# Adding the experts' rows to x by accumulating DMAs, and one more expert by one-hot products

## The chip, the cores and the metric

The kernel runs on one core of a Trainium2 chip. The core has a matrix engine (TensorE, PE in the profile), a vector engine (VectorE, DVE), an activation engine (ScalarE, ACT), a general engine (GpSimd, POOL) and an engine that issues transfers (SyncE, SP). Each engine runs its own queue of instructions; semaphores order them among each other. Transfers run on 16 DMA engines, whichever engine issued them. The metric is the device time of one execution in microseconds, the median of several runs.

## The reference

One decoder layer in float32 over 512 tokens of width 1024: a front part (attention and a recurrent mixer), an output projection, then a mixture of experts and a last norm. Only the last part matters here:

```python
logits = (xf @ router_w + router_b)          # 512 tokens, 32 experts
top_val, top_idx = lax.top_k(logits, 4)      # each token goes to 4 experts
gates = softmax(top_val)
# for each expert e, over the tokens that chose it:
gu = xb @ mlp1_w[e] + mlp1_b[e]              # 1024 -> 2048
act = (up + 1.0) * gate * sigmoid(1.702 * gate)
y = act @ mlp2_w[e] + mlp2_b[e]              # 1024 -> 1024
# the output:
x = x + sum over the token's 4 experts of gate * y
return rmsnorm(x, final_norm_w)
```

## The kernel before, in words

The kernel has three blocks: `front`, `output_and_route`, and `experts`. The change is in the third, but for one line.

**Rounds.** `experts` handles up to 128 rows of each expert in one round, and there can be four rounds, for the case that an expert was chosen by more than 128 tokens. Every engine has a `run(r)` with its whole work of a round. The helper `rounds` (L1382 to 1386) loops over four rounds; in each it loads a flag from the tile `flags` into a register (L1384) and branches over the body if the flag is not set (L1385). With these inputs one round is run and three are skipped. SP alone runs its first round (`rest(0)`, L1423) outside that loop.

**An expert's pieces.** The weights come in as pieces of 1 MB: eight pieces for the product up, four (`DOWN`) for the product down. SP loads them into six slots of `raw` (L1395), each as soon as VectorE has finished with the piece six before. ScalarE rounds each piece to float32r (`split`, L1491, into `w_pieces_hi`), VectorE takes the rest (`split`, L1597, into `w_pieces_lo`), and TensorE makes three products of parts for each piece (L1775, L1778 for up, L1796, L1801 for down). The turn `b` of the steady loop does the product down of expert b-2 and the product up of expert b. After the loop the product down of expert 30 (turn 32, into banks 4 and 5) and of expert 31 (turn 33, into banks 0 and 1) are left.

**Rows in and out.** GpSimd gathers an expert's rows of the normed x (`gather`, L1445), and scatters the gated results `ys` (written by ScalarE, L1511) into rows of `y_dram`, called expert_rows in the profile (`scatter`, L1457), at row 4 * token + (which of the token's four choices). After each scatter it waits for the landing (L1459). `y_dram` was filled with zeros in `front` (L344). `SCATTERED` is 31: experts 0 to 30 are scattered. Expert 31 isn't: its 128 rows are brought to their tokens on TensorE. The one-hot matrix of its tokens (`sel`, made by VectorE with an is_equal, L1603) is turned (L1852), copied to `sel_t` (L1568), and multiplied with the high and low part of the gated result (`y_hi` by ScalarE L1577, `y_lo` by VectorE L1701, products in `choose`, L1875), on top of the bias of the product down (`down_bias`, L1870).

**The end.** When the last scatter has landed, SP (which waits at L1410) loads 16 tiles of 512 KB from `y_dram`, four for each of the four tiles of 128 tokens (L1416), into `raw` and `o_t`. For each tile of tokens, in the order `LAST_ROWS` = 0, 3, 1, 2, VectorE adds in five instructions the four loads, x, and the sum in PSUM (L1717, L1720, L1723, L1726, L1728); ScalarE squares and sums the row (L1581) and takes the root (L1583); VectorE inverts it (L1707) and scales by it and by the weight (`finish`, L1711); SP stores the tile (L1419). `finish(n-1)` stands behind the five additions of tile n. After that SP (L1420) and VectorE (L1732) wait for the stores and GpSimd (L1477) for the last scaling, and only then do they skip the three other rounds. The block ends with a DRAIN on each engine and a barrier (L171).

Of the kernel before, what the change touches and what calls it, by code (L numbers as in the profile page):

```python
# [19 lines left out]
F32 = mybir.dt.float32  # L20
# [3 lines left out]
ALU = mybir.AluOpType  # L24
# [3 lines left out]
P = 128  # L28
# [16 lines left out]
SCATTERED = EXPERTS - 1  # L45
# [990 lines left out]
def output_and_route(nc, d, sb, sem, st, g, con, ident, psum, bank):  # L1036
# [124 lines left out]
    def _(dve):  # L1161
# [81 lines left out]
        nc.vector.tensor_tensor(rank[:, :, INDEXED - 1:INDEXED], which[:, :, EXPERTS - 1:EXPERTS], ranks[:, :, EXPERTS - 1:EXPERTS], ALU.add)  # L1243
# [89 lines left out]
def experts(nc, d, sb, sem, st, g, con, ident, psum, bank, out):  # L1333
# [31 lines left out]
    s_row = [[sem(f"row_loaded{t}_{k}") for k in range(4)] for t in range(NT)]  # L1365
    s_fw, s_add, s_sum, s_ss, s_sd, s_rs, s_o, s_out = (sem(n) for n in ("final_w_loaded", "rows_added", "rows_summed", "x3_squared",
                                                                         "x3_deviation", "x3_rstd", "out_ready", "out_stored"))
    sel_t = xh[:, 0:NT, :].rearrange("p a b -> p (a b)")
    y_hi, y_lo = (a[:].rearrange("p a b -> p (a b)") for a in (ah, al))
    fw, final = xg, (uu, sg, av, ys)  # L1370
    gate_last = tab[:, EXPERTS - 1, 2:3]
    rows_v = y_dram.rearrange("(t p k) n -> t p k n", p=P, k=4)
    last_banks = {0: 2, 3: 6, 1: 4, 2: 0}

    def row(t, k):

        return raw[:, 2 * t + k // 2, k % 2, :] if t < 3 else o_t[:, 2 * k:2 * k + 2, :].rearrange("p a s -> p (a s)")
# [4 lines left out]
    def rounds(eng, run):  # L1382
        with eng.Fori(0, ROUNDS) as r:
            flag = eng.value_load(flags[0:1, bass.ds(r, 1)])  # L1384
            with eng.If(flag == 1):  # L1385
                run(r)

    @block.sync
    def _(sp):
# [7 lines left out]
        def rest(r):  # L1397
# [22 lines left out]
            sp.wait_ge(s_out, (r * NT + NT) * 16)  # L1420
            sp.sem_inc(s_part, 1)

        rest(0)  # L1423
        with sp.Fori(1, ROUNDS) as r:
            flag = sp.value_load(flags[0:1, bass.ds(r, 1)])
            with sp.If(flag == 1):
                for p in range(DOWN, DOWN + RAW):
                    load(r, 0, p)
                rest(r)

    @block.gpsimd
    def _(pool):
# [29 lines left out]
        def run(r):  # L1462
# [14 lines left out]
            pool.wait_ge(s_o, r * NT + NT)  # L1477
            pool.sem_inc(s_part, 1)

        rounds(pool, run)  # L1480

    @block.scalar
    def _(act):
# [50 lines left out]
        def run(r):  # L1534
# [32 lines left out]
            act.wait_ge(s_st, r + 1)  # L1567
            nc.scalar.activation(sel_t, bank(7), ACT.Copy).then_inc(s_selt, 1)  # L1568
# [6 lines left out]
            y_out(r, b - 2, b)  # L1575
            act.wait_ge(s_used, r * STREAM + (STREAM + RING))
            nc.scalar.activation(y_hi, psum[:, 0:2, :].rearrange("p b n -> p (b n)"), ACT.Copy, scale=gate_last).then_inc(s_y, 1)  # L1577
            nc.scalar.activation(stat[:, 52:53], con("eps"), ACT.Sqrt)
            for n, t in enumerate(LAST_ROWS):
                act.wait_ge(s_sum, r * NT + (n + 1))  # L1580
                nc.scalar.activation(row(t, 0), final[t][:], ACT.Square, accum_out=stat[:, 40 + t:41 + t]).then_inc(s_ss, 1)  # L1581
# [3 lines left out]
        rounds(act, run)  # L1585

    @block.vector
    def _(dve):
# [66 lines left out]
        def run(r):  # L1655
# [39 lines left out]
            for p in range(DOWN - 1):  # L1695
                split(r, b + 1, p)
            a_lo(r, b - 1, 1, 7)
            split(r, b + 1, DOWN - 1)
            nc.vector.tensor_scalar(rank[:], rank[:], float(-P), None, ALU.add).then_inc(s_round, 1)
            dve.wait_ge(s_y, r * EXPERTS + (EXPERTS + 1))  # L1700
            nc.vector.scalar_tensor_tensor(y_lo, psum[:, 0:2, :].rearrange("p b n -> p (b n)"), gate_last, y_hi.bitcast(F32),  # L1701
                                           ALU.mult, ALU.subtract).then_inc(s_yl, 1)

            def finish(n):
# [6 lines left out]
                nc.vector.scalar_tensor_tensor(final[t][:], final[t][:], stat[:, 48 + t:49 + t], fw[:], ALU.mult, ALU.mult).then_inc(s_o, 1)  # L1711

            for n, t in enumerate(LAST_ROWS):
                f = final[t][:]
                for k in range(2):
                    dve.wait_ge(s_row[t][k], r * 16 + 16)
                nc.vector.tensor_tensor(f, row(t, 0), row(t, 1), ALU.add).then_inc(s_add, 1)  # L1717
                dve.wait_ge(s_row[t][2], r * 16 + 16)
                dve.wait_ge(s_add, r * 4 * NT + (4 * n + 1))
                nc.vector.tensor_tensor(f, f, row(t, 2), ALU.add).then_inc(s_add, 1)  # L1720
                dve.wait_ge(s_hot, r * NT + (n + 1))
                summed = psum[:, last_banks[t]:last_banks[t] + 2, :].rearrange("p b n -> p (b n)")
                nc.vector.tensor_tensor(x[:, t, :], summed, x[:, t, :], ALU.add).then_inc(s_add, 1)  # L1723
                dve.wait_ge(s_row[t][3], r * 16 + 16)
                dve.wait_ge(s_add, r * 4 * NT + (4 * n + 2))
                nc.vector.tensor_tensor(f, f, row(t, 3), ALU.add).then_inc(s_add, 1)  # L1726
# [11 lines left out]
    def _(pe):  # L1738
# [89 lines left out]
        def run(r):  # L1828
# [52 lines left out]
            for t in LAST_ROWS[:3]:  # L1881
                down_bias(t)
# [47 lines left out]
```

## Time and profile before

| what | value |
|---|---|
| median of 3 runs | 1749.18 us (1747.82 to 1750.51) |
| the profiled execution | 1748.68 us |
| its span, first to last instruction | 1746.8 us |
| TensorE busy | 1589.4 us, 91% of the span |
| VectorE busy | 1423.9 us, 82% |
| ScalarE busy | 1052.6 us, 60% |
| first instruction of `experts` / last of VectorE | 519.2 us / 1737.8 us |

The span is what the profile shows of one execution; the time of that execution has 1.9 us more around it. Where a stretch is full on TensorE, a delay of TensorE is a delay of everything behind it; in the last 45 us the queue that sets the end changes several times, so that stretch has to be read instruction by instruction.

### The profile page before, as it was taken

Reading aid. Unit: us, or ns where it says so; the run is one execution under the profiler, and the core shown is the slowest. Engines: PE = TensorE matmul, PEld = TensorE weight load, DVE = VectorE, ACT = ScalarE, POOL = GpSimd, SP = SyncE. Lnnn points to the kernel's source line nnn. Section 1 sums busy time; section 2 is a strip of 40 time slices with the busy share of each in tenths; the row PEclk is TensorE's granted clock in tenths of the full one; section 3 lists DMA queues with packets and bytes.
Section 4 is the critical chain, followed back from the end, with each engine's and each line's share of the span. In section 5 each row is a group of like instructions: output and inputs, shape, how many; then the busy total and the mean of one; then the engine's idle time right before and its main releaser. Section 6 shows DMA issues by size and latency. Waiting matters only on the chain.

```text
span 1746.8 us, 28600 instructions
## 1 busy us (share of the span) xinstructions
PE 1589.4 (91%) x10300; PEld 1279.4 (73%) x10301; DVE 1423.9 (82%) x1296; ACT 1052.6 (60%) x968; POOL 309.6 (18%) x208
## 2 busy tenths in 40 slices
PE   5888889886877999999999999999999999999991
PEld 5666657665665788888888888888888888888880
DVE  4757667475637799999999999999999999999976
ACT  5434242322335677777777777777777777777761
POOL 6200000000001031122211222122321213222210
PEclk9999899998878999999999999999999999999995
DMA  5610011000547699999999999999999999999956
GB/s 185 242 38 25 26 37 38 26 1 2 208 169 287 241 363 370 361 357 367 358 381 372 349 375 369 371 368 347 368 363 368 352 359 368 364 359 361 358 207 248
DMA packets 100824, 467.62 MB, mean 268 GB/s; under 512 B 12734, under 2 KB 39374, under 8 KB 51488
## 3 DMA queue, kind: packets, MB, share of 16 engines
q1 hardware_dynamic: 88336, 438.11, 66.3%
q0 software_dynamic: 12432, 28.70, 4.4%
q8 instruction: 43, 0.70, 0.2%
q14 instruction: 13, 0.11, 0.0%
HBM read 454.88 MB, written 28.84 MB: 277 GB/s over the span
## 4 chain that ended last, share of the span: by engine, by line
PE 65%; DVE 1%; issue 1%; DMA 1%; ACT 1%; SPq 0%; DVEq 0%; POOL 0%; POOLq 0%; ACTq 0%
PE psum L1775 27%; PE psum L1778 13%; PE psum L1796 13%; PE psum L1801 6%; PE psum L1767 2%; PE psum L1757 2%; PE psum L1787 1%; PE psum L1748 1%; DMA o_t<-expert_rows 1%; ACT w_pieces_hi L1491 0%; DMA expert_rows<-ys,this_i 0%; DMA xg<-h_rows,gath_i 0%; DVE xl L1614 0%; DVE w_pieces_lo L1597 0%; SPq L1416 0%
## 5 line engine op out<-in xcount | busy, mean ns | idle before, releaser
L1597 DVE TENSOR_TENSOR w_pieces_lo<-w_pieces,w_pieces_hi 128x2048 fp32r<-128x2048 f32 x384 | 870.7, 2287 | 91.0 <-ACT w_pieces_hi L1491 91.0
L1491 ACT ACTIVATE w_pieces_hi<-w_pieces 128x2048 fp32r<-128x2048 f32 x384 | 736.7, 1919 | 296.7 <-PE psum L1778 225.2
L1775 PE MATMUL psum<-w_pieces_hi,xh 128*128 128x512 f32 x1024 | 293.6, 409 | 1.1 <-DVE xl L1614 1.1
L1775 PE MATMUL psum<-w_pieces_hi,xl 128*128 128x512 f32 x1024 | 277.5, 393 | 0.0
L1778 PE MATMUL psum<-w_pieces_lo,xh 128*128 128x512 f32 x1024 | 277.3, 393 | 0.0
L1775 PEld LDWEIGHTS psum<-w_pieces_hi,xl 128*128 128x128 f32 x1024 | 193.7, 189 | 43.4
L1778 PEld LDWEIGHTS psum<-w_pieces_lo,xh 128*128 128x128 f32 x1024 | 193.4, 189 | 43.1
L1775 PEld LDWEIGHTS psum<-w_pieces_hi,xh 128*128 128x128 f32 x1024 | 182.4, 190 | 42.9 <-issue 12.0
L1457 POOL DMA_INDIRECT expert_rows<-ys,this_i x31 | 156.8, 5059 | 269.0 <-ACT ys L1511 269.0
L1796 PE MATMUL psum<-w_pieces_hi,ah 128*128 128x512 f32 x512 | 160.7, 395 | 0.0
L1796 PE MATMUL psum<-w_pieces_hi,al 128*128 128x512 f32 x512 | 158.2, 390 | 0.0
L1801 PE MATMUL psum<-w_pieces_lo,ah 128*128 128x512 f32 x512 | 136.9, 389 | 0.0
L1796 PEld LDWEIGHTS psum<-w_pieces_hi,al 128*128 128x128 f32 x512 | 96.1, 188 | 20.2
L1801 PEld LDWEIGHTS psum<-w_pieces_lo,ah 128*128 128x128 f32 x512 | 96.1, 188 | 20.1
L358 ACT ACTIVATE pall<-psum 128x512 f32<-128x512 f32 x26 | 15.5, 595 | 154.9 <-PE psum L780 154.9
L1796 PEld LDWEIGHTS psum<-w_pieces_hi,ah 128*128 128x128 f32 x512 | 93.7, 188 | 18.1 <-DVE al L1620 0.3
L780 PE MATMUL psum<-h_hi_sb,w_hi_sb 128*128 128x512 f32 x208 | 91.6, 441 | 9.9 <-ACT pall L358 9.9
L1445 POOL DMA_INDIRECT xg<-h_rows,gath_i x33 | 81.2, 2460 | 28.4 <-POOL gath_i L1442 28.4
L780 PE MATMUL psum<-h_hi_sb,w_lo_sb 128*128 128x512 f32 x208 | 85.1, 409 | 0.0
L780 PE MATMUL psum<-h_lo_sb,w_hi_sb 128*128 128x512 f32 x208 | 84.7, 407 | 0.0
L1442 POOL CAST gath_i<-index_table 128x1 int32 (+1 forms) x33 | 7.3, 220 | 367.3 <-PE psum L1757 364.0
L1114 POOL MEMSET rb<- 32x1 f32 x1 | 0.1, 88 | 384.4 <-POOLq L158 384.4
(371 smaller groups left out, 1976.1 us busy)
## 6 DMA issues: line engine op xcount, KB each, us to landing
w_pieces<-in_mlp_w SPq DMA_DIRECT2D x384, 1024.0 KB, 7.1
w_raw<-in_w_in SPq DMA_DIRECT2D x26, 512.0 KB, 3.8
expert_rows<-o_t POOLq DMA_DIRECT2D x4, 2048.0 KB, 14.2
w_pieces<-expert_rows SPq DMA_DIRECT2D x12, 512.0 KB, 13.5
w_pieces<-in_w_out SPq DMA_DIRECT2D x8, 512.0 KB, 9.7
chunk_work<-in_x SPq DMA_DIRECT2D x4, 512.0 KB, 5.5
x<-in_x SPq DMA_DIRECT2D x4, 512.0 KB, 13.8
h_rows<-w_pieces POOLq DMA_DIRECT2D x4, 512.0 KB, 2.9
```

Of the source, the lines that this page charges most:

```text
L780: last = nc.tensor.matmul(o, w[:, n % 3, k, :], h[:, k, :], start=k == 0 and m == 0, stop=k == KT - 1 and m == 2)
L1445: nc.gpsimd.indirect_dma_start(xg[:], None, g["h2_dram"], bass.IndirectOffsetOnAxis(gath_i[:, 0:1], 0), bounds_check=S - 1, oob_is_err=Fal ...
L1457: nc.gpsimd.indirect_dma_start(g["y_dram"], bass.IndirectOffsetOnAxis(this_i[:, 0:1], 0), ys[:], None, bounds_check=4 * S - 1, oob_is_err= ...
L1491: nc.scalar.activation(hi[:, p % RING], raw[:, raw_slot(b, p)].rearrange("p r n -> p (r n)"), ACT.Copy).then_inc(s_hi, 1)
L1597: nc.vector.tensor_tensor(lo[:, p % RING], raw[:, raw_slot(b, p)].rearrange("p r n -> p (r n)"), hi[:, p % RING].bitcast(F32), ALU.subtrac ...
L1748: last = nc.tensor.matmul(bank(4, 0, 4), sel[:, t, :], info[:, t, bass.ds(m, 1), :].rearrange("p a c -> p (a c)"), start=t == 0, stop=t == ...
L1757: last = nc.tensor.transpose(bank(7, k * P, k * P + P), xg[:, (4 * q + k) * P:(4 * q + k + 1) * P], ident)
L1767: last = nc.tensor.transpose(bank(into, k * P, k * P + P), rows[:, k // 2, k % 2, :], ident)
L1775: nc.tensor.matmul(bank(c), a[:, k, :], hi[:, p % RING, c * 512:(c + 1) * 512], start=False, stop=False)
L1778: last = nc.tensor.matmul(bank(c), xh[:, k, :], lo[:, p % RING, c * 512:(c + 1) * 512], start=False, stop=k == KT - 1)
L1796: nc.tensor.matmul(bank(into + c), a[:, 2 * p + r2, :], hi[:, p % RING, r2 * D + c * 512:r2 * D + (c + 1) * 512], start=p == 0 and r2 == 0 ...
L1801: last = nc.tensor.matmul(bank(into + c), ah[:, 2 * p + r2, :], lo[:, p % RING, r2 * D + c * 512:r2 * D + (c + 1) * 512], start=False, sto ...
```

## The change

Four things change.

1. **Expert 30 as expert 31.** `SCATTERED` becomes 30. The result of expert 30 isn't scattered; ScalarE and VectorE write its high part into `xl` and its low part into a slot of `w_pieces_lo`. A second one-hot matrix is made (one more L1603-like instruction on VectorE behind the first split of turn 33), turned (four more transposes on TensorE behind the first piece of turn 33, into bank 2) and copied (ScalarE), and each tile of tokens gets four more products (16 in all).
2. **Accumulating DMAs.** SP's 16 loads go. GpSimd issues 16 transfers with `accum_op=ALU.add` that add the rows of `y_dram` to `x` in SBUF directly. They start when the last weight piece has landed. The four of one tile of tokens (k = 0 to 3) follow each other, each waiting for the landing of the one before; the four tiles run side by side.
3. **The end on VectorE.** Of the five additions of a tile one is left (PSUM plus x into x).
4. **Rounds.** Round 0 is run outside the loop and without a flag on every engine; what a second round needs first is done in `again(r)` only if there is one (waiting for the stores, blanking the gates, and filling `y_dram` with zeros again). The wait for the stores moves behind the skipped rounds on SP, and VectorE and GpSimd no longer wait for anything before they skip.

```diff
-SCATTERED = EXPERTS - 1
+SCATTERED = EXPERTS - 2
...
+    sel_t = [xh[:, 4 * n:4 * n + 4, :].rearrange("p a b -> p (a b)") for n in range(2)]
+    y_hi = [a[:].rearrange("p a b -> p (a b)") for a in (xl, ah)]
+    y_lo = [lo[:, 0, 0:D], al[:].rearrange("p a b -> p (a b)")]
...
-    def rounds(eng, run):
-        with eng.Fori(0, ROUNDS) as r:
+    def rounds(eng, run, again=None):
+        run(0)
+        with eng.Fori(1, ROUNDS) as r:
             flag = eng.value_load(flags[0:1, bass.ds(r, 1)])
             with eng.If(flag == 1):
+                if again:
+                    again(r)
                 run(r)
...
-            sp.wait_ge(s_scat, (r * SCATTERED + SCATTERED) * 16)
-            sp.sem_inc(s_part, 1)
-            for t in LAST_ROWS:
-                if t < 3:
-                    sp.wait_ge(s_lo, r * STREAM + (STREAM + 2 * t + 2))
-                for k in range(4):
-                    sp.dma_start(row(t, k), rows_v[t, :, k, :]).then_inc(s_row[t][k], 16)
             for n, t in enumerate(LAST_ROWS):
                 sp.wait_ge(s_o, r * NT + (n + 1))
                 sp.dma_start(out[0, t * P:(t + 1) * P, :], final[t][:]).then_inc(s_out, 16)
-            sp.wait_ge(s_out, (r * NT + NT) * 16)
...
+        sp.wait_ge(s_out, NT * 16)
...
-            prepare(r, EXPERTS - 2)
-            scatter(r, EXPERTS - 2)
-            pool.wait_ge(s_tx, (r * TURNS + EXPERTS) * 2 + 2)
+            pool.wait_ge(s_tx, (r * TURNS + EXPERTS) * 2 + 3)
             pool.sem_inc(s_part, 1)
             nc.gpsimd.dma_start(fw[:], d["final_norm_w"].to_broadcast([P, D])).then_inc(s_fw, 16)
-            pool.wait_ge(s_hot, r * NT + NT)
+            last_slot = raw_slot(EXPERTS + 1, DOWN - 1)
+            pool.wait_ge(s_raw[last_slot], (r * (STREAM // RAW) + raw_fills(EXPERTS + 1, DOWN - 1)) * 16)
+            pool.sem_inc(s_part, 1)
+            for k in range(4):
+                for t in LAST_ROWS:
+                    if k:
+                        pool.wait_ge(s_row[t], (r * 4 + k) * 16)
+                        pool.sem_inc(s_part, 1)
+                    nc.gpsimd.dma_start(x[:, t, :], rows_v[t, :, k, :], accum_op=ALU.add).then_inc(s_row[t], 16)
...
             for p in range(DOWN - 1):
                 split(r, b + 1, p)
+                if p == 0:
+                    dve.wait_ge(s_st, r * 2 + 1)
+                    nc.vector.tensor_tensor(sel[:], con("slot").rearrange("p (a n) -> p a n", a=1).to_broadcast([P, NT, P]),
+                                            rank[:, :, b - 1:b].to_broadcast([P, NT, P]), ALU.is_equal).then_inc(s_sel31, 1)
...
             for n, t in enumerate(LAST_ROWS):
-                f = final[t][:]
...
-                nc.vector.tensor_tensor(f, row(t, 0), row(t, 1), ALU.add).then_inc(s_add, 1)
...
-                nc.vector.tensor_tensor(f, f, x[:, t, :], ALU.add).then_inc(s_sum, 1)
...
                 dve.wait_ge(s_hot, r * NT + (n + 1))
+                dve.wait_ge(s_row[t], r * 64 + 64)
+                nc.vector.tensor_tensor(x[:, t, :], psum[:, last_banks[t]:last_banks[t] + 2, :].rearrange("p b n -> p (b n)"), x[:, t, :],
+                                        ALU.add).then_inc(s_add, 1)
                 if n:
                     finish(n - 1)
             finish(NT - 1)
-            dve.wait_ge(s_out, (r * NT + NT) * 16)
```

## Rows read from the trace of the kernel before

**Rows 1.** The page: busy time of the engines, share of the span, instructions.

```profile
PE 1589.4 (91%) x10300; PEld 1279.4 (73%) x10301; DVE 1423.9 (82%) x1296; ACT 1052.6 (60%) x968; POOL 309.6 (18%) x208
```

**Rows 2.** Windows: start:end, length, busy of each engine, PEclk, DMA share, GB/s.

```profile
635.00:1670.00 1035.00, 1035.00 (x4826) 844.94 (x4825) 964.79 (x633) 773.68 (x547) 247.74 (x144) 1.00 0.95 364
...
1684.00:1701.00 17.00, 17.00 (x79) 13.94 (x78) 13.39 (x9) 9.31 (x8) 0.99 (x1) 1.00 0.06 22
...
1704.00:1726.00 22.00, 3.56 (x16) 2.60 (x14) 18.08 (x17) 3.52 (x8) 0.53 (x1) 0.67 1.02 399
```

**Rows 3.** The chain that ended last, its end in order of time: start, us, what.

```profile
1696.04 5.21 DMA expert_rows<-ys,this_i
...
1703.88 10.07 DMA o_t<-expert_rows
```

**Rows 4.** Waits of SP's own queue after 1690 us: total, times, longest.

```profile
SPq L1411 <- DMA expert_rows<-ys,this_i: 24.0, 1, 24.0
```

**Rows 5.** Timeline of the end: start, us, engine, line, operation, size, idle before.

```profile
1701.80 1.52 PE L1870 MATMUL psum<-down_bias,gates_turned 128*128 128x512 f32 x6
1702.00 1.12 ACT L1577 ACTIVATE ah<-psum,index_table 128x1024 fp32r<-128x1024 f32 x1 [6.85 <-PE psum L1801]
...
1733.57 1.23 DVE L1728 TENSOR_TENSOR av<-av,x 128x1024 f32<-128x1024 f32 x1
...
1734.83 1.06 ACT L1581 ACTIVATE w_pieces<-av 128x1024 f32<-128x1024 f32 x1 [5.84 <-DVE av L1728]
...
1736.54 1.28 DVE L1711 SCALAR_TENSOR_TENSOR av<-av,stat,xg 128x1024 f32<-128x1024 f32 x1
1737.85 0.33 SPq L1419 DMA_DIRECT2D out<-av  x1
```

**Rows 6.** SP's piece loads after 1660 us; then issues, KB, us to landing.

```profile
L1395 SPq DMA_DIRECT2D w_pieces<-in_mlp_w x7: 327/328/338, 1659.8 to 1676.9; - x7
...
w_pieces<-in_mlp_w SPq DMA_DIRECT2D x1, 1024.0 KB, 5.4
...
out<-av SPq DMA_DIRECT2D x1, 512.0 KB, 2.6
```

**Rows 7.** Lines of GpSimd's DMA instructions: ns min/median/max, first and last start.

```profile
L1457 POOL DMA_INDIRECT expert_rows<-ys,this_i x31: 994/5194/5210, 612.2 to 1696.0; - x31
...
L344 POOL DMA_DIRECT2D expert_rows<-o_t x4: 743/759/860, 50.6 to 52.9; - x4
```

**Rows 8.** Timeline, one scatter's issue in the steady loop, and VectorE's instructions beside it.

```profile
1657.64 5.19 POOL L1457 DMA_INDIRECT expert_rows<-ys,this_i  x1 [8.14 <-ACT ys L1511]
...
1655.27 6.69 DVE L1597 TENSOR_TENSOR w_pieces_lo<-w_pieces,w_pieces_hi 128x2048 fp32r<-128x2048 f32 x3
```

**Rows 9.** Turn 33's wait (timeline), four transposes (chain), one selection (its line).

```profile
1681.23 0.44 PE psum L1852 x4
...
1696.23 0.30 PEld L1796 LDWEIGHTS psum<-w_pieces_hi,ah 128*128 128x128 f32 x2 [0.35 <-DVE al L1620]
...
L1603 DVE TENSOR_TENSOR sel<-cst,rank x34: 680/683/702, 520.7 to 1654.7; 128x512 fp32r<-128x512 f32 x34
```

**Rows 10.** The chain at the start of the block: the first flag, on VectorE.

```profile
519.67 0.05 DVEq L1383
...
520.53 0.05 DVEq L1656
```

**Rows 11.** Lines after the last scaling: SP's loop over rounds, the DRAINs of the block's end.

```profile
L1424 SPq COMPARE_BRANCH  x3: 40/45/45, 1741.8 to 1743.8; - x3
L1424 SPq MOVE  x1: 29/29/29, 1740.5 to 1740.5; - x1
...
L171 POOLq DRAIN  x1: 5359/5359/5359, 1741.3 to 1741.3; - x1
...
L171 DVEq DRAIN  x1: 17/17/17, 1744.1 to 1744.1; - x1
```

More of the change, by code:

```diff
@@ L1242, in _ @@
         nc.vector.tensor_tensor(rank[:, :, 0:EXPERTS], which[:], ranks, ALU.add)
-        nc.vector.tensor_tensor(rank[:, :, INDEXED - 1:INDEXED], which[:, :, EXPERTS - 1:EXPERTS], ranks[:, :, EXPERTS - 1:EXPERTS], ALU.add)
+        nc.vector.tensor_tensor(rank[:, :, INDEXED - 1:INDEXED], which[:, :, EXPERTS - 2:EXPERTS - 1], ranks[:, :, EXPERTS - 2:EXPERTS - 1], ALU.add)
         chain(nc.vector.tensor_reduce(r1[:, 20:21], bank(1, NT * EXPERTS, (NT + 1) * EXPERTS), AX.X, ALU.max))
@@ L1468, in run, with again @@
                 scatter(r, b - 2)
-            prepare(r, EXPERTS - 2)
-            scatter(r, EXPERTS - 2)
-            pool.wait_ge(s_tx, (r * TURNS + EXPERTS) * 2 + 2)
+            pool.wait_ge(s_tx, (r * TURNS + EXPERTS) * 2 + 3)
             pool.sem_inc(s_part, 1)
             nc.gpsimd.dma_start(fw[:], d["final_norm_w"].to_broadcast([P, D])).then_inc(s_fw, 16)
-            pool.wait_ge(s_hot, r * NT + NT)
+            last_slot = raw_slot(EXPERTS + 1, DOWN - 1)
[7 more added lines that the diff above has]
+                    nc.gpsimd.dma_start(x[:, t, :], rows_v[t, :, k, :], accum_op=ALU.add).then_inc(s_row[t], 16)
+        def again(r):
+            pool.wait_ge(s_o, r * NT)
             pool.sem_inc(s_part, 1)
             nc.gpsimd.memset(turned[:].bitcast(F32), 0.0).then_inc(s_blank, 1)
-            pool.wait_ge(s_o, r * NT + NT)
+            nc.gpsimd.memset(xg[:], 0.0).then_inc(s_z, 1)
+            pool.wait_ge(s_z, r + 1)
             pool.sem_inc(s_part, 1)
-        rounds(pool, run)
+            for n in range(4):
+                nc.gpsimd.dma_start(y_dram[n * S:(n + 1) * S, :].rearrange("(a p) n -> p a n", p=P),
+                                    xg[:].rearrange("p (a n) -> p a n", a=1).to_broadcast([P, S // P, D])).then_inc(s_wiped, 16)
+            pool.wait_ge(s_wiped, r * 64)
+            pool.sem_inc(s_part, 1)
+        rounds(pool, run, again)
     @block.scalar
@@ L1731, in run, with again @@
             finish(NT - 1)
-            dve.wait_ge(s_out, (r * NT + NT) * 16)
+        def again(r):
+            dve.wait_ge(s_out, r * NT * 16)
             dve.sem_inc(s_part, 1)
-        rounds(dve, run)
+        rounds(dve, run, again)
     @block.tensor
@@ L1803, in down_piece, with turn_choice @@
             last.then_inc(s_used, 1)
+        def turn_choice(into):
+            for t in range(NT):
+                last = nc.tensor.transpose(bank(into, t * P, t * P + P), sel[:, t, :].bitcast(F32), ident)
+            last.then_inc(s_st, 1)
         def down(r, b, turn):
@@ L1850, in run @@
             pe.wait_ge(s_xl, (r * TURNS + b) * 2 + 1)
-            for t in range(NT):
-                last = nc.tensor.transpose(bank(7, t * P, t * P + P), sel[:, t, :].bitcast(F32), ident)
-            last.then_inc(s_st, 1)
+            turn_choice(7)
             pe.sem_inc(s_tx, 1)
@@ L1866, in run @@
                 down_piece(r, b + 1, p, 0)
+                if p == 0:
+                    pe.wait_ge(s_sel31, r + 1)
+                    turn_choice(2)
             def down_bias(t):
```

85 lines of the change are left out of this document (45 added, 40 removed).

## The prediction, made before the changed kernel was run

> **What bounds the kernel now.** I read the page first, then the windows, then the chain and the timeline of the last 60 us. On the page TensorE has 91% of the span [rows 1]. The windows say where that holds: over 1035 us of the steady loop TensorE is busy all the time, the DMA engines 0.95 of it [rows 2]. Nothing in the change touches that loop, so it can only gain at the two edges: where `experts` starts, and behind the last weight piece.
>
> The chain of the end shows what sets it. The last scatter is issued at 1696.0 and takes 5.2 us to land; SP has waited 24.0 us for it; only then do the 16 loads begin, and the chain runs through them for 10 us [rows 3, 4]. Behind that VectorE works without a gap: five additions and a scaling for each tile, up to 1737.8 [rows 3, 5]. And from 1684 to 1701 the DMA engines are almost idle (0.06), though 30 of the 31 scatters have landed: the one before the last was issued at 1657.6, and GpSimd waits for each landing before it goes on [rows 2, 8]. Last, the span goes on for 9.0 us after VectorE's last scaling ends at 1737.82. SP begins its skipped rounds at 1740.5 and ends them at 1743.9; GpSimd's DRAIN starts at 1741.3 and takes 5.4 us, and it ends the span [rows 11].
>
> **The change part by part**, in the clock of the profile before.
>
> *Start of the block.* The flag of round 0 goes. On the chain it is the stretch from 519.67 to 520.53 on VectorE [rows 10], and the other engines load the same flag. Gain 0.85 us. The steady loop behind it is full on TensorE, so the gain is kept.
>
> *Turn 33.* VectorE has one more selection, 0.68 us, before the low part that TensorE already waits 0.35 us for; TensorE has four more transposes there, some 0.44 us as the four of L1852. TensorE now comes 0.44 later to a datum that is 0.68 later: a delay of 0.68 us [rows 9]. ScalarE's result for expert 30 keeps its length, and its copy of the second choice is short beside 6.85 us of idle time [rows 5].
>
> *Products of the end.* Six matmuls there go at 1.52 us less one's tail, 0.226 us each [rows 5]. The 16 new ones cost 3.6 us. If only they counted, the first bias product starts at 1702.5, 18 products (6 bias, 12 for expert 30) end at 1706.6, six high products of expert 31 at 1707.9, and the first tile's sum is there at 1708.5, the fourth's at 1711.5. VectorE then needs for each tile an addition (1.2) and an inverse with the scaling (1.45), ScalarE 1.5 between them (from 1734.83 to the inverse, 1.71 to the scaling); played out in that order the last scaling ends at 1719.8. That is the floor, if the rows are in x by then.
>
> *The rows.* The last piece is issued at 1676.9 and takes 5.4 us [rows 6]. GpSimd then needs one issue, 0.76 us [rows 7], so data flows at about 1684 (the final weight is read just before). The 16 transfers hold 8.4 MB. What an accumulating transfer costs no row shows. Bounds: 16 plain loads ran at 399 to 410 GB/s with the DMA engines at 1.02 of their time, 1.28 us for 512 KB [rows 2]. Less than that an accumulating one can't take, as it moves these bytes too. From above: GpSimd's DMA instruction at its longest, 5.2 us each [rows 7]. In between: to add, a transfer has to read x as well as the row, two reads for one write. The plain loads are already at the limit of engines that read each byte once, so I take twice, 2.56 us, the row it is nearest to being two plain passes. 16 x 2.56 = 41 us. Three others are in flight while one lands and its successor is issued, so the waits within a tile cost nothing as long as landing and issue take less than 7.7 us; if that cover went, each of four steps would show about 2 us. The last rows are then in x at 1684 + 41 + 0.6 = 1725.6.
>
> The Trainium skill (Collectives: The Full Stack, "The bandwidth ceiling") has a price for adding while copying: 62.28 GB/s without and 32.35 with it, a factor of 1.93. No row here shows it. By it one transfer would be 2.47 us and the time 1.4 us less than I give.
>
> *After the last rows.* The last tile's addition waits 0.2 us for the scaling before it, and from the start of the last addition to the end of the last scaling the timeline has 4.25 us (1733.57 to 1737.82) [rows 5]. So the last scaling ends at 1730.1, 7.8 us earlier than now. The four additions per tile that go are worth nothing by themselves: the transfers end later than VectorE would.
>
> *Behind the last scaling.* SP issues the store in 0.36 us, and now skips its rounds while it lands (2.6 us [rows 6]); three skips take 3.35 us [rows 11]. VectorE skips beside it in 3.6 us. With the barrier 4.2 us in place of 9.0. GpSimd issues its last transfer when the one of k = 2 has landed, 10 us before the last rows; skips (3.3) and DRAIN (5.4) end before 1726, or at 1731 if the DRAIN has to wait for the landing: covered by the 8.6 us after it. If it had no cover it would cost up to 5 us.
>
> *Sum.* With t for one accumulating transfer: 1684 + 16 t + 0.6 + 4.45 + 4.2 - 0.85 = 1692.4 + 16 t, and not under 1719.8 + 4.2 - 0.85 = 1723.2. At t = 2.56 the span is 1733.4, 13.4 us under 1746.8. The profiled execution took 1748.68, so 1735.3; the median of the runs lies 0.5 us above that execution, so I predict **1736 us**.
>
> **A rule against it.** In the steady loop a scatter's issue at 1657.64 lasts 5.19 us, while the one at 1696 takes 0.99. In those 5.19 us VectorE runs L1597, which reads two tiles in SBUF, back to back up to 1661.96, and the issue ends 0.87 us after it [rows 7, 8]. So GpSimd's issue seems to wait for VectorE's instruction to end. In 1684 to 1698.4 VectorE is almost full with the same line [rows 2]. The Trainium skill (SBUF — State Buffer, "Who interferes with whom") says that a VectorE instruction with two SBUF inputs contends with a GpSimd one that reads SBUF, and the trace agrees for the scatter, which reads its indices. The same section takes descriptor generation to need only writes. By the one the accumulating issues stall, by the other they don't.
>
> **The rivals.**
> 1. *The sum is nearly free.* t up to 1.92 us: the rows are in x before VectorE and TensorE are ready, and the floor holds: span 1723.2, time 1725.5. For it: two reads may overlap where one read and one write do now. Against: a DMA share of 1.02 with plain loads [rows 2].
> 2. *GpSimd's issues stall in the splits.* 5.2 us for each of the issues until 1698.4, three of them, then 13 transfers at 2.56: the rows are in at 1732.3, the time 1743. For it [rows 8]; against: a plain transfer has no indices to read, and three in flight hide part.
> 3. *The accumulating transfer becomes the bound: slower.* If each takes 5.2 us, be it in GpSimd's issue or in the DMA engines, the span is 1692.4 + 83.2 = 1775.6 and the time 1778. It decides from 16 t = 54.4, t = 3.4 us, 2.65 times a plain load. For it: nothing in this profile shows an adding transfer near full rate. Against: GpSimd's four direct transfers of 2 MB were issued in 0.74 to 0.86 us each [rows 7].
>
> **How the numbers follow.** Forecast with t near twice (2.2 to 3.0 us; 1730 to 1743): 0.50, rival 2 with its 1743 among them at 0.08 more. Rival 1 and what lies between it and 2.2 us: 0.20. Rival 3 from t = 3.6 up: 0.14. Between (t of 3.0 to 3.6): 0.08, most of it within 0.2% of before (3.5 us, about what a measurement of this kernel can tell from no change). That gives faster 0.80, same 0.06, slower 0.14. The range that leaves out no more than 2 in 10 reaches from the floor, 1724, over the forecast to just beyond no change, 1752; the forecast's own is 1730 to 1743.
>
> **What would show it.** The first transfer into x issued at 1682 to 1684, DMA share near 1 for some 41 us from there, half of 400 GB/s if the profile counts each byte once; last landing at about 1725. VectorE idle from about 1704 to 1717, waiting for DMA. One addition of 1.22 us per tile. Last scaling at 1729, the span ending 4 us behind it, no GpSimd DRAIN in the end. GpSimd's issues at 0.6 to 0.8 us each (5 would be rival 2 or 3). The start of the steady loop 0.85 us earlier. The prediction is wrong if t is off: each tenth of a microsecond in it moves the time by 1.6 us.

## The result, and the profile after

The changed kernel takes **1740.14 us** in the median of four runs (1738.89 to 1741.58); the kernel before took 1749.85 beside it. The ratio is 0.9946, with a 95% interval of 0.9929 to 0.9964: faster by half a per cent, 9.7 us. The forecast was 1736, a gain of 13; about three quarters of it came, within both ranges. The profiled execution took 1740.51 us, its span 1738.7.

Read it as before: first the busy times on the page, with the line on the new transfers.

```profile
PE 1595.0 (92%) x10320; PEld 1283.9 (74%) x10321; DVE 1408.4 (81%) x1282; ACT 1051.9 (61%) x968; POOL 312.1 (18%) x220
...
x<-expert_rows POOLq DMA_DIRECT2D x16, 512.0 KB, 9.5
```

The windows (start:end, length, busy of each engine, PEclk, DMA share, GB/s) beside those of [rows 2]:

```profile
635.00:1670.00 1035.00, 1035.00 (x4825) 845.04 (x4825) 965.06 (x634) 774.08 (x547) 239.58 (x143) 1.00 0.95 364
1687.00:1687.50 0.50, 0.50 (x4) 0.42 (x3) 0.50 (x1) 0.00 (x0) 0.50 (x3) 1.00 0.55 66
...
1692.00:1696.00 4.00, 4.00 (x21) 3.33 (x20) 4.00 (x3) 4.00 (x5) 1.73 (x2) 1.00 1.07 209
1712.00:1716.00 4.00, 0.24 (x2) 0.00 (x0) 0.00 (x0) 0.00 (x0) 1.74 (x2) 0.84 1.07 212
1716.00:1720.00 4.00, 0.00 (x0) 0.00 (x0) 0.00 (x0) 0.00 (x0) 0.87 (x1) 0.50 1.06 212
...
1727.50:1728.00 0.50, 0.00 (x0) 0.00 (x0) 0.50 (x2) 0.13 (x1) 0.00 (x0) 0.50 1.00 197
1728.00:1728.50 0.50, 0.00 (x0) 0.00 (x0) 0.50 (x1) 0.00 (x0) 0.00 (x0) 0.50 0.36 98
```

The steady loop is as it was. The new transfers' data flows from 1687 (half a microsecond earlier the DMA engines moved nothing) to 1728. From 1692 on the DMA engines are full, at 1.06 of their time, but move only 210 GB/s, where plain loads moved 399 [rows 2]. Whether TensorE runs beside them (1692) or nothing does (1716), the rate is the same. And from 1712.24 to 1722.44 no engine but GpSimd works at all: everything waits for the rows.

The chain that ended last, its end in order of time (start, us, what), beside [rows 3]:

```profile
1677.55 7.36 DMA w_pieces<-in_mlp_w
...
1685.49 0.58 POOL x L1475
1686.07 8.48 DMA x<-expert_rows
...
1695.10 9.40 DMA x<-expert_rows
...
1705.05 9.40 DMA x<-expert_rows
...
1715.00 9.80 DMA x<-expert_rows
...
1724.90 1.23 DVE x L1743
...
1732.98 1.28 DVE av L1738
```

Last weight piece, four adding transfers of one tile behind each other, then VectorE: the path that the forecast was made along. The chain follows the second tile's rows, since behind its addition VectorE has work without a wait; the last rows land at 1729.7 (issued at 1720.13, 9.6 us to landing) and are added at 1730.02, so they are only 0.3 us ahead of VectorE. GpSimd's timeline (start, us, engine, line, operation, size, idle before) has the transfers one by one:

```profile
1679.20 0.58 POOL L1466 DMA_DIRECT2D xg<-in_final_norm_w  x1 [15.76 <-PEq L1875]
1685.49 3.62 POOL L1475 DMA_DIRECT2D x<-expert_rows  x4 [5.70 <-DMA w_pieces<-in_mlp_w]
1692.62 0.86 POOL L1475 DMA_DIRECT2D x<-expert_rows  x1 [3.50 <-DMA x<-expert_rows]
1695.10 0.86 POOL L1475 DMA_DIRECT2D x<-expert_rows  x1 [1.62 <-DMA x<-expert_rows]
...
1720.13 0.87 POOL L1475 DMA_DIRECT2D x<-expert_rows  x1 [1.61 <-DMA x<-expert_rows]
```

From 1692.62 to 1720.13 eleven steps take 27.51 us: 2.50 us for a transfer. Each issue costs GpSimd 0.87 us, so it waits for landings two thirds of the time. VectorE's timeline, beside [rows 5]:

```profile
1704.37 1.28 DVE L1724 SCALAR_TENSOR_TENSOR al<-psum,index_table,ah 128x1024 fp32r<-128x1024 f32 x1 [3.45 <-ACT ah L1589]
1722.44 1.23 DVE L1743 TENSOR_TENSOR x<-psum,x 128x1024 f32<-128x1024 f32 x1 [16.79 <-DMA x<-expert_rows]
1724.90 1.23 DVE L1743 TENSOR_TENSOR x<-psum,x 128x1024 f32<-128x1024 f32 x1 [1.24 <-DMA x<-expert_rows]
...
1730.02 1.22 DVE L1743 TENSOR_TENSOR x<-psum,x 128x1024 f32<-128x1024 f32 x1
...
1732.98 1.28 DVE L1738 SCALAR_TENSOR_TENSOR av<-x,stat,xg 128x1024 f32<-128x1024 f32 x1
```

The last scaling ends at 1734.26, where it ended at 1737.82 before; behind it come 4.4 us, where 9.0 came [rows 5, 11]. So of the 8.1 us by which the span is shorter, 3.6 were earned ahead of the last scaling and 4.5 behind it. The waits (engine, tile, line, releaser: us in all, times, longest) say what is late now:

```profile
POOL x L1475 <- DMA x<-expert_rows: 21.4, 12, 3.5
DVE x L1743 <- DMA x<-expert_rows: 18.0, 2, 16.8
...
PEld psum L1814 <- DVE al L1636: 0.5, 1, 0.5
```

And the rows of the new line itself and of GpSimd's DRAIN, beside [rows 7, 11]:

```profile
L1475 POOL DMA_DIRECT2D x<-expert_rows x16: 863/872/1952, 1685.5 to 1720.1; - x16
...
DMA to landing us min/median/max: 6.6/9.5/12.4
```

```profile
L171 POOLq DRAIN  x1: 7023/7023/7023, 1726.0 to 1726.0; - x1
```

### The profile page after: what moved, and what is told of

Read it like the earlier page. It is cut to its first block, busy times and chain, and to the rows that moved or that the text cites. A ratio compares the mean times of both kernels' runs of the same rounds, so it can differ in the third digit from the quotient of the medians.

```text
span 1738.7 us, 28043 instructions
## 1 busy us (share of the span) xinstructions
PE 1595.0 (92%) x10320; PEld 1283.9 (74%) x10321; DVE 1408.4 (81%) x1282; ACT 1051.9 (61%) x968; POOL 312.1 (18%) x220
## 4 chain that ended last, share of the span: by engine, by line
PE 65%; DMA 3%; DVE 1%; ACT 1%; issue 0%; POOL 0%; POOLq 0%; PEldq 0%; ACTq 0%; DVEq 0%
PE psum L1793 27%; PE psum L1796 13%; PE psum L1814 13%; PE psum L1819 6%; DMA x<-expert_rows 2%; PE psum L1785 2%; PE psum L1775 2%; PE psum L1805 1%; PE psum L1766 1%; DMA w_pieces<-in_mlp_w 0%; DVE w_pieces_lo L1613 0%; ACT w_pieces_hi L1501 0%; DMA xg<-h_rows,gath_i 0%; DVE x L1743 0%; DVE xl L1630 0%
## 5 line engine op out<-in xcount | busy, mean ns | idle before, releaser
L1452 POOL DMA_INDIRECT expert_rows<-ys,this_i x30 | 151.8, 5059 | 248.0 <-issue 248.0
```

Of the source, the lines that this page charges most:

```text
L1452: nc.gpsimd.indirect_dma_start(g["y_dram"], bass.IndirectOffsetOnAxis(this_i[:, 0:1], 0), ys[:], None, bounds_check=4 * S - 1, oob_is_err= ...
```

## The experiments

The theory after this profile: the adding transfers set the end by their rate in the DMA engines, about 2.5 us each from the landing of the last weight piece. Rivals: the pace is set by GpSimd's issues and the waits between the four of a tile; the late start is made by the final weight's load; the gain is that of the rounds alone. Ratios are to the kernel before on the same chip; they can lie 0.001 (2 us) off the quotient of the two medians that stand beside them, so both are given. One execution's front can lie a microsecond or two off another's, whatever stands behind it (the low part of expert 31, at 1704.37 above, stands between 1702.46 and 1706.37 in the kernels below). So inside a profile I measure from there.

**1. The rounds alone.** The kernel before, with only the new `rounds` and what goes with it.

```diff
-    def rounds(eng, run):
-        with eng.Fori(0, ROUNDS) as r:
+    def rounds(eng, run, again=None):
+        run(0)
+        with eng.Fori(1, ROUNDS) as r:
...
```

> The kernel before with part 4 alone: round 0 outside the loop, the waits for the stores moved behind the skipped rounds; rows, additions and experts as before. My theory: the flag at the block's start is 0.85 us of the chain, and behind VectorE's last scaling 9.0 us shrink to about 4.4, so the span falls from 1746.8 to about 1741.4 and the time by 5.4 us. Rival: the gain of the whole change is all in rows and additions, then this is within 1 us of before, because SP's three skips and the barrier take what GpSimd's DRAIN took.

Measured: 1746.06 us to 1749.13, ratio 0.9979 (0.9969 to 0.9989). The last scaling ends at 1737.82, to the hundredth where it was, and the span ends 4.4 us behind it in place of 9.0. So 3.7 us by the ratio (1.9 to 5.4 by its interval; 3.1 in the medians) have nothing to do with the rows. That is under the 5.4 us expected. The flag's gain does show at the start, where the block's first product comes 14.42 us after its first memset, before 15.24; but the low part of expert 31 stands at 1703.35, no earlier than the 1703.15 of before, so what the start gained is not seen again at the end of this profile. That VectorE and GpSimd skip early costs nothing, though GpSimd's DRAIN is now longer than anyone's work:

```profile
L171 POOLq DRAIN  x1: 9022/9022/9022, 1702.7 to 1702.7; - x1
```

Its 16 plain loads give the rate to compare with:

```profile
1708.00:1720.00 12.00, 0.00 (x0) 0.00 (x0) 10.62 (x10) 1.46 (x4) 0.00 (x0) 0.63 1.02 407
```

407 GB/s at a share of 1.02 against 212 at 1.06: the adding transfer costs 1.92 plain ones. The Trainium skill (Collectives: The Full Stack, "The bandwidth ceiling") has a factor of 1.93 for a copy that adds, and puts it down to two reads for one write; the trace agrees with the factor.

**2. The same transfers without the addition.** The 16 transfers copy into x, so x holds the last row only.

```diff
-                    nc.gpsimd.dma_start(x[:, t, :], rows_v[t, :, k, :], accum_op=ALU.add).then_inc(s_row[t], 16)
+                    nc.gpsimd.dma_start(x[:, t, :], rows_v[t, :, k, :]).then_inc(s_row[t], 16)
```

> The changed kernel with its 16 transfers into x as plain copies (no addition, so x holds the last row only; everything else alike, same engine, same waits). My theory: an adding transfer takes twice the DMA time of a plain one (2.5 us against 1.28), so without the addition the DMA rate goes from 211 to some 410 GB/s, the rows are there before TensorE's last products, and the time falls by 12 to 14 us to the floor near 1727. Rival: GpSimd's issue and the wait for each landing set the pace; then the transfers still start every 2.5 us and the time stays within 2 us of the changed kernel.

Measured: 1726.58 us, ratio 0.9863 (0.9847 to 0.988): 13.6 us under the changed kernel. GpSimd's timeline and then VectorE's:

```profile
1685.67 2.11 POOL L1475 DMA_DIRECT2D x<-expert_rows  x4 [5.02 <-DMA w_pieces<-in_mlp_w]
...
1690.82 0.53 POOL L1475 DMA_DIRECT2D x<-expert_rows  x1 [3.04 <-DMA x<-expert_rows]
...
1695.12 0.53 POOL L1475 DMA_DIRECT2D x<-expert_rows  x1 [0.73 <-DMA x<-expert_rows]
1696.41 0.53 POOL L1475 DMA_DIRECT2D x<-expert_rows  x1 [0.75 <-DMA x<-expert_rows]
...
1709.14 0.53 POOL L1475 DMA_DIRECT2D x<-expert_rows  x1 [2.92 <-DMA x<-expert_rows]
```

```profile
1710.18 2.48 DVE L1743 TENSOR_TENSOR x<-psum,x 128x1024 f32<-128x1024 f32 x2 [3.65 <-DMA x<-expert_rows]
```

With the same queue, the same order and the same waits the cadence is 1.25 to 1.3 us at its shortest and 1.67 us in the mean (eleven steps from 1690.82 to 1709.14), where it was 2.50. The rival that the issues and landings set the pace of 2.50 us falls. The first tile's rows land at 1710.09 here, about when TensorE has that tile's sum (its last products for it are among the six that start at 1709.34), and behind them VectorE has no wait for rows. What is left is the floor of the forecast, in effect: 1726.6 measured, 1725.5 worked out.

**3. Twelve adding transfers.** The fourth row of each token is left out of the sum.

```diff
-            for k in range(4):
+            for k in range(3):
```

> The changed kernel with 12 adding transfers in place of 16 (k = 3 is left out, so that choice is missing from the sum). Theory: the time is linear in the number of transfers at 2.5 us each: 10 us less, about 1730. Rival: another queue behind them is nearly as late; then the gain stops short, and at 4 us less or fewer the forecast's floor was too low.

Measured: 1731.91 us, ratio 0.99 (0.9884 to 0.9917). The span is 9.1 us shorter, and the low part of expert 31 stands 0.6 later, so 9.7 us for four transfers: 2.4 each. The medians give 8.2 us, 2.1 each. VectorE's first addition:

```profile
1713.36 1.23 DVE L1743 TENSOR_TENSOR x<-psum,x 128x1024 f32<-128x1024 f32 x1 [7.13 <-DMA x<-expert_rows]
```

The wait of 16.8 us became 7.1, by the same 9.7. Between twelve and sixteen, the two numbers that were run, the time goes with the number of adding transfers, and 7.1 us of the wait are still left at twelve.

**4. The final weight behind the sixteen.** In the changed kernel its load of 0.5 MB is in flight when the last weight piece is.

```diff
-            nc.gpsimd.dma_start(fw[:], d["final_norm_w"].to_broadcast([P, D])).then_inc(s_fw, 16)
... the wait for the last piece and the sixteen adding transfers
+            nc.gpsimd.dma_start(fw[:], d["final_norm_w"].to_broadcast([P, D])).then_inc(s_fw, 16)
```

> The changed kernel with the load of the final norm's weight issued behind the 16 adding transfers in place of ahead of them. Theory: it held the DMA engines 1.3 us and delayed the last weight piece (7.4 us to landing against 5.4 before), so the adding transfers start 1.3 to 2 us earlier and the time falls by as much. Rival: its landing now comes after the last row and VectorE's first scaling waits for it, 0 to 1 us in all.

Measured: 1744.76 us, ratio 0.9977 (0.9964 to 0.999), 4.6 us above the changed kernel in the medians (the two intervals just touch, at 0.9964). The last piece landed at 1685.7, 7.9 us after its issue at 1677.8: the piece lands no earlier without the weight's load, and my theory of the late start falls. In the first experiment, which has none of the new transfers, it took 7.6 us. Instead VectorE got a new wait:

```profile
1731.73 1.28 DVE L1738 SCALAR_TENSOR_TENSOR uu<-x,stat,xg 128x1024 f32<-128x1024 f32 x1 [4.82 <-DMA xg<-in_final_norm_w]
```

The load was issued at 1721.47 and needed 10 us: it stood behind the four adding transfers in flight, 4 x 2.5 us.

**5. The changed kernel again**, as the base of the next three on one chip.

> The changed kernel as it is, on the chip of the next three, as their reference: about 1740 us, 9.4 us under the kernel before.

Measured: 1741.18 us, ratio 0.9956 (0.9941 to 0.9971).

**6. Rows of some tiles by plain loads.** For the tiles in `PLAIN`, SP loads the four rows of each token (into `o_t` and free slots of `raw`) and VectorE adds them to x in the time in which it waits now. Three kernels: tile 3 alone, tiles 3 and 0, all four (no adding transfer left: the new expert 30 and the new rounds, with loads and additions on VectorE as before, but into x and with two of the additions ahead of the low part of expert 31).

```diff
+            for t in PLAIN:
...
+                for k in range(4):
+                    sp.dma_start(row(t, k), rows_v[t, :, k, :]).then_inc(s_plain[t], 16)
...
-                for t in LAST_ROWS:
+                for t in [t for t in LAST_ROWS if t not in PLAIN]:
...
+                nc.vector.tensor_tensor(x[:, t, :], row(t, k), x[:, t, :], ALU.add).then_inc(s_pa, 1)
```

> The changed kernel, but the four rows of tile 3 are loaded by SP as plain copies into o_t and added by VectorE (two additions before and two behind its low part of expert 31, where it is idle for 3.5 and 16.8 us); 12 adding transfers are left. Theory: only DMA time counts here: four transfers at 2.5 us become four at 1.28, mostly in time in which the DMA engines are idle or busy anyway, so the last rows come some 5 to 8 us earlier and the time falls by as much, to 1732 to 1735. Rival: VectorE's four additions (4.6 us) and the mixing of the loads with the last piece take it back; then the time is within 2 us of the changed kernel.

> As the one with four plain rows, but tiles 3 and 0 are loaded plainly (tile 0 into the first two weight slots when their splits are done) and VectorE adds eight; 8 adding transfers are left. Theory: DMA work behind the last piece is 8 x 1.28 + 8 x 2.5 = 30 us in place of 40 and VectorE's eight additions lie in its idle time up to 1713; the last scaling moves from 1734 to about 1724 and the time to about 1729 to 1731. Rival: with two tiles left only two adding transfers are in flight, so each landing and issue (6.6 us for a lone one) shows; then it is no better than with four plain rows.

> The changed kernel with no adding transfer at all: SP loads the 16 rows plainly as in the kernel before, but with expert 30 by one-hot products and the new rounds; VectorE adds each to x (5 additions a tile). This is parts 1 and 4 of the change alone. Theory: VectorE is the bound again: from 1705.7 some 14 additions at 1.15, four scalings and PSUM additions at 2.6 and 1.7 at the end give a last scaling at 1734, by chance what the changed kernel has; the time is within 2 us of it, so the adding transfers themselves earned nothing. Rival: the adding transfers are what made the change fast; then this is 4 us or more slower.

Measured: 1734.55 us (ratio 0.9922, 0.9901 to 0.9943), 1733.84 (0.9913, 0.9888 to 0.9937) and 1741.43 (0.9958, 0.9945 to 0.9972). The last is the surprise: without a single adding transfer the kernel is as fast as with sixteen (1741.18 on the same chip). VectorE's timeline there:

```profile
1701.34 2.47 DVE L1750 TENSOR_TENSOR x<-o_t,x 128x1024 f32<-128x1024 f32 x2
...
1708.67 5.00 DVE L1750 TENSOR_TENSOR x<-w_pieces,x 128x1024 f32<-128x1024 f32 x4
...
1733.57 1.28 DVE L1766 SCALAR_TENSOR_TENSOR av<-x,stat,xg 128x1024 f32<-128x1024 f32 x1
```

From 1704.89 it works without a gap of over half a microsecond to 1734.85; the rows wait for it, not it for the rows. So with all rows added by DMA the DMA engines are the bound and VectorE idles for 18 us; with none VectorE is, and the DMA engines idle. The best lies between. With eight rows' worth by each way neither should be the bound, but the second kernel is no clear gain over the first; its window and its chain show why:

```profile
1708.00:1720.00 12.00, 6.25 (x28) 4.85 (x26) 10.71 (x10) 2.78 (x6) 2.60 (x3) 0.87 0.84 138
```

```profile
1709.64 7.76 DMA x<-expert_rows
...
1717.95 7.07 DMA x<-expert_rows
```

With two tiles there are only two chains of adding transfers. They move 138 GB/s at a share of 0.84, which is a transfer of 512 KB each 3.8 us in place of 2.5; the issues say the same (3.9 us, five steps from 1698.33 to 1717.95). Each transfer takes 7 to 8 us from issue to landing with only one other beside it, and GpSimd waits 22.6 us for six landings. Three chains already come near the full rate: in the first of these kernels, with tile 3 alone by plain loads, the window is this, and its issues stand 2.5 us apart.

```profile
1708.00:1720.00 12.00, 5.98 (x27) 4.62 (x25) 2.65 (x3) 0.00 (x0) 3.52 (x4) 0.87 1.06 204
```

**7. Adds ahead of the last pieces.** The last scatter lands at about 1670, 15 us before the changed kernel issues its first adding transfer. Here the 16 don't wait for the last weight piece, only for the last scatter; the final weight's load, not in this cut, comes behind them.

```diff
-            pool.wait_ge(s_raw[last_slot], (r * (STREAM // RAW) + raw_fills(EXPERTS + 1, DOWN - 1)) * 16)
-            pool.sem_inc(s_part, 1)
```

> The changed kernel with its adding transfers issued as soon as the last scatter has landed (about 1671), not after the last weight piece (about 1685); the final weight's load is issued behind them. Theory: until 1684 the DMA engines are 0.9 and more busy with weight pieces, so the same DMA work has to be done either way; the adding transfers only take time from the pieces. The rows are there at best 2 us earlier, and the late load of the final weight, behind the last adding transfers, costs its 5 us again unless they end before 1724: time between 1738 and 1746. Rival: the wait for the last piece is what costs; then the last rows come up to 14 us earlier and the time falls to the floor, about 1727.

Measured: 1739.73 us, ratio 0.9945 (0.993 to 0.9961), no different from the changed kernel. The first transfer is issued at 1670.30, the last at 1713.59, and TensorE never waits for a piece; but the final weight is late again:

```profile
1724.26 1.28 DVE L1735 SCALAR_TENSOR_TENSOR uu<-x,stat,xg 128x1024 f32<-128x1024 f32 x1 [4.31 <-DMA xg<-in_final_norm_w]
```

**8. The same with the final weight's load behind the first four.**

```diff
+                if not k:
+                    pool.wait_ge(s_tx, (r * TURNS + EXPERTS) * 2 + 3)
+                    pool.sem_inc(s_part, 1)
+                    nc.gpsimd.dma_start(fw[:], d["final_norm_w"].to_broadcast([P, D])).then_inc(s_fw, 16)
```

> As the one with the adding transfers ahead of the last pieces, but the final weight's load goes out behind the first four of them and not behind all 16. In that run the last row came some 4.6 us earlier than in the changed kernel (last issue 1713.6 against 1720.1, with a block that began 1.9 us earlier), and VectorE waited 4.3 us for the weight. Theory: without that wait the 4.3 us show as time: about 1735 to 1736, 4 to 5 us under the changed kernel, so the wait for the last weight piece costs that much. Rival: the first four and the weight push the last pieces back so far that TensorE waits; then it is no faster than 1739.

Measured: 1736.5 us, ratio 0.9932 (0.9912 to 0.9952), with no wait for that weight. The interval overlaps that of the changed kernel, the medians are 3.6 us apart. The profiles agree: from the low part of expert 31 (1703.99 and 1704.37) to the first addition it is now 13.95 us, before 18.07:

```profile
1717.94 1.22 DVE L1741 TENSOR_TENSOR x<-psum,x 128x1024 f32<-128x1024 f32 x1 [12.66 <-DMA x<-expert_rows]
```

By the profiles, waiting for the last piece costs the changed kernel 4 us, and no more than that, though the transfers start 14 us later for it (1685.49, here 1671.23): here they share full DMA engines with the weight pieces until the last piece lands at 1691.7, and eleven of the 16 are issued from 1687 on.

**9. Two tiles plain, the others in halves.** As the second kernel of 6, but each adding transfer cut into two of 512 columns, so that four chains run again; and the same without the wait for the last piece.

```diff
-                    nc.gpsimd.dma_start(x[:, t, :], rows_v[t, :, k, :], accum_op=ALU.add).then_inc(s_row[t], 16)
+                    nc.gpsimd.dma_start(x[:, t, h * 512:h * 512 + 512], rows_v[t, :, k, h * 512:h * 512 + 512],
+                                        accum_op=ALU.add).then_inc(s_row[t][h], 16)
```

> The kernel with eight plain rows, its 8 adding transfers cut into halves of 512 columns, so that four chains are in flight and not two. Theory: with two in flight the DMA engines moved 138 GB/s of the 211 that four gave, because landing and issue (3 to 4 us of idle time of GpSimd's queue before each) were not covered; with four chains they are, the last rows come 5 us earlier, the time falls from 1734 to about 1729. Rival: 2 KB runs cost the DMA engines more than 4 KB runs and GpSimd's issues double, so it is no faster than 1734.

> The kernel with halves, its adding transfers no longer waiting for the last weight piece, issued right behind the final weight's load (about 1682 in place of 1689). Theory: the DMA engines are full until 1697 in any case, so 0 to 2 us are gained, and the last piece has 8 us to spare. Rival: the last pieces come late, TensorE waits, and it is slower than with the wait.

Measured: **1731.04 us** to 1750.00, ratio 0.9904 (0.988 to 0.9927), and 1731.14 (0.9897, 0.9874 to 0.992). Both beat the kernel before and the changed one: the interval of the first ends at 0.9927, just below the 0.9929 at which that of the changed kernel begins. The windows and VectorE's timeline of the first:

```profile
1690.00:1700.00 10.00, 9.96 (x47) 7.87 (x46) 10.00 (x8) 5.47 (x5) 2.59 (x3) 1.00 1.08 299
1704.00:1716.00 12.00, 7.48 (x33) 5.85 (x32) 11.14 (x11) 3.29 (x6) 6.14 (x7) 0.91 1.01 163
```

```profile
1707.38 5.01 DVE L1751 TENSOR_TENSOR x<-w_pieces,x 128x1024 f32<-128x1024 f32 x4
1712.49 2.36 DVE L1778 TENSOR_TENSOR x<-psum,x 128x1024 f32<-128x1024 f32 x2
...
1715.53 1.28 DVE L1767 SCALAR_TENSOR_TENSOR uu<-x,stat,xg 128x1024 f32<-128x1024 f32 x1
...
1722.36 1.28 DVE L1767 SCALAR_TENSOR_TENSOR av<-x,stat,xg 128x1024 f32<-128x1024 f32 x1
```

VectorE has no wait for rows any more and ends at 1723.64. That is why starting the transfers earlier gives nothing here. Against whole transfers for the same two tiles the gain is 3.0 us from the selection (the last one-hot matrix) to the last scaling in the profiles (35.7 and 32.7 us); in the medians 2.8 us and by the ratios 1.6, whose intervals overlap, so it is likely and not proved. Halves reach 163 GB/s in the second window with the DMA engines at 1.01, not 212: the rate of smaller adding transfers alone was not measured.

## Why the prediction was nearly right, step by step

**The path was right.** Last piece, 16 adding transfers side by side in four chains, last addition, last scaling, 4 us behind it. Experiments 2 and 3 show that the transfers' rate carries it: as plain copies they leave the floor, and without four of them 8 to 10 us go.

**The adding transfer, the main unknown, was right**: 2.56 us taken. The data of the 16 flows from 1687.1 to 1728.1, by the half-microsecond windows, and that is 41.0 us for 16, or 2.56 each, slower at the start and 2.50 by the cadence. Leaving out four gives 2.4 in the profiles and 2.1 in the medians. That the second decimal comes out is luck: it was a choice of twice a plain load, in a range of 2.2 to 3.0.

**The step that was mis-sized is the start of the data.** The prediction said "The last piece is issued at 1676.9 and takes 5.4 us", and had data flowing at 1684, 1683.15 with the shorter start. It flows at 1687.1, 3.95 later. 1.05 of it is the front of this execution: the first memset of the block stands at 520.23 and stood at 519.18, in code that is not changed. 0.4 is the steady loop. 2.0 is the last piece: 7.36 us on the chain where I had taken 5.4 [rows 6]. The rest, 0.5, lies between the landing (1684.91) and the data: 2.2 us, of which 0.5 pass before GpSimd issues. The prediction named 0.76 us for that stretch and by its rounding to 1684 allowed 1.7. Those 5.4 us were one landing of one execution, the last piece's own. The six pieces issued in the 16 us before it had a median of 6.6, and in the other kernels that have no adding transfers beside it the last one took 6.6 to 9.0 us. The DMA engines are full there: from 1660 to 1676 both kernels show it (a share of 1.00 to 1.01 before, 0.94 to 1.01 after). In the window behind that, the kernel before shows a share of 0.61 and 255 GB/s, the changed one this:

```profile
1676.00:1684.00 8.00, 8.00 (x39) 6.63 (x38) 6.18 (x4) 4.59 (x3) 0.58 (x1) 1.00 0.95 350
```

That is 0.76 MB more in 8 us. The final weight's load, which the kernel before issues only at 1702, is 0.52 of it; but the kernel of experiment 1 has no load of that weight there either, and shows 0.78 and 294 GB/s. A median over the pieces of the end would have been the better term. The final weight's load isn't what delays it (experiment 4), nor are the adding transfers (7.6 us in experiment 1, which has none). Why the last piece took only 5.4 us in that one execution stays open.

**The landing of the last rows** was put 0.6 us behind their data. The data ends at 1728.1 and the last transfer lands at 1729.7 (issued at 1720.13, 9.6 us to landing): 1.6 us, 1.0 more than forecast.

**Sum of the differences**: 3.95 at the start and 1.0 at the landing make 4.95 at the last rows. 0.1 more comes at the last scaling (4.55 for 4.45) and 0.25 behind it (4.45 for 4.2): 5.3 us, the whole of 1738.7 against 1733.4. In the medians only 4 us of it show, since the gap between the profiled execution and the median was taken as 0.5 us and was -0.4.

**The small steps.** The block's first product comes 14.42 us after the memset, before 15.24: 0.82 gained, 0.85 forecast. The low part of turn 33 is waited for 0.5 us where it was 0.35 [rows 9], so VectorE's extra selection is what delays, as argued. TensorE's last product ended at 1712.24; the forecast's 1711.5, 0.85 earlier for the flag and 1.45 later for this execution's front and loop, is 1712.1. One addition takes 1.22 to 1.23. GpSimd's DRAIN took 7.0 us, not 5.4, from 1726.0 to 1733.0, and was covered by VectorE's last microseconds, as said.

**The rivals.** Rival 1, nearly free, needed at most 1.92 us for a transfer; experiment 2 shows that for a plain copy (1.67 in the mean), and the addition takes it away. Rival 2 is refuted: the issues of 1685 to 1698 take 0.87 us in the median beside the same splits in which a scatter took 5.19 [rows 8], the longest 1.95. The Trainium skill (SBUF — State Buffer, "Who interferes with whom") takes descriptor generation to need only writes, and by it these issues would not stall; the trace agrees, and the row of the scatter was the wrong one to carry over. It was also read too simply: the scatter at 1696.04 took 0.99 us although VectorE ran the same two-input line beside it from 1696.10 to 1698.38, so a scatter doesn't always wait for such an instruction. Rival 3 needed 3.4 us for a transfer. With two chains in flight 3.8 was measured (experiment 6), more than that; with a third chain it is 2.5, so the number of chains is what keeps this rival away. The prediction named this cover and was right to count on it.

**What I had not asked.** The prediction priced the new way against the old as written, not against the old way with the rest of the change. Experiment 6 shows that the comparison is even: 1741.18 us with 16 adding transfers and 1741.43 with none, on one chip. The whole change gave 9.7 us at first and 7.1 when it was run again (experiment 5). The rounds gave 3.1 to 3.7 of them, and the adding transfers nothing over loads and additions on VectorE. What is left over, 3.7 us by the ratios of experiment 6's third kernel and experiment 1, comes with expert 30, whose scatter no longer is the last thing to land: SP's loads of rows start at 1678.5 there, before at 1701.3. Expert 30 was not run alone, and that kernel also orders the additions anew, so how the 3.7 us divide is not shown.

## What to carry to other kernels

Adding in the DMA engines halves their rate here (212 GB/s for 407), so what it takes off a vector engine it pays for in DMA time. Let it carry only as much as the vector engine can't do in the same time. With half of the rows by each way, in four chains, the end came 7 to 10 us earlier than with all or nothing. Count the independent chains: two were too few (138 GB/s), three and four gave 204 and 212. Put every small load that is needed afterwards ahead of the adding transfers. Before pricing a change against the kernel as it is, price its independent parts (here the skipped rounds) by themselves.

## What the runs showed of the hardware

- Adding transfers from DRAM into SBUF, four in flight, run at 209 to 212 GB/s with the DMA engines at 1.06 of their time, plain ones at 407 at 1.02 (experiment 1). One costs GpSimd 0.87 us to issue, a plain one of the same shape 0.53 (experiment 2).
- Two chains of 512 KB reach 138 GB/s, three 204 (both experiment 6), four 212.
- A plain load of 0.5 MB issued behind four adding transfers lands after 10 us (experiment 4), and after 16.7 when weight pieces run beside them too (experiment 8); ahead of them it took 6.9.
- GpSimd's DRAIN at the end of the block took 5.4 us before, 7.0 after, and between 5.3 (experiment 6, third kernel) and 10.2 us (experiment 7) in the others. What sets it stays open; it ended the span only in the kernel before.
- A weight piece of 1 MB lands after 5.0 to 9.0 us at the end of the loop, with the DMA engines full; with adding transfers beside it (experiment 8) the last one took 14.5 us, and TensorE still had it in time.
